# Five edits between the output projection and the experts of a hybrid encoder layer

## The reference, cut to what matters

```python
x = x + token_mixer(rmsnorm(x, attn_norm_g), w_in, ...)     # ends in  merged @ w_out
xn = rmsnorm(x, ffn_norm_g)
pg_top, g_sel = top_k(softmax(xn @ w_rg + b_rg), 1)         # 1 of 4 groups
pe_top, e_sel = top_k(softmax((xn @ w_re + b_re)[g_sel]), 2)  # 2 of its 8 experts
gate = pg_top * pe_top / sum(pe_top)
h = silu(xb @ w1[e]) * (xb @ w3[e])                         # 1024 -> 512
y = (h @ w2[e]) * gate                                      # 512 -> 1024
return rmsnorm(x + sum(y), final_norm_g)
```

## Time and profile before

| what | value |
|---|---|
| median of three runs | 1255.5 us |
| profiled execution, its time | 1254.98 us |
| profiled execution, its span | 1253.3 us |
| PE busy | 1114.9 us, 89% of the span |
| DVE busy | 510.9 us, 41% |
| ACT busy | 421.9 us, 34% |
| DMA moved | 308.89 MB |

### The profile page before, as it was taken

One profiled execution on the slowest core, in us unless ns is written; L12 is line 12 of the kernel. 1 busy time (PEld: TensorE's weight loads), 2 busy tenths in 40 slices (PEclk: granted clock), 3 DMA queues, 4 the chain that ended last, 5 costly groups with the idle time before them and its releaser, 6 DMA issues.

```text
span 1253.3 us, 15692 instructions
## 1 busy us (share of the span) xinstructions
PE 1114.9 (89%) x5136; PEld 684.8 (55%) x5136; DVE 510.9 (41%) x837; ACT 421.9 (34%) x658; POOL 229.9 (18%) x275
## 2 busy tenths in 40 slices
PE   5899999999988977999995699999999999898960
PEld 4688888888855645788784233333333333333320
DVE  5511111113237746755346244343515453424128
ACT  5322222223145655533114133333333342424222
POOL 0111101110007001000000033333323332423220
PEclk9899999999998967999996799999999999999985
DMA  8633331711160001746548989999999999999816
GB/s 320 233 118 118 112 114 50 284 47 45 50 252 2 1 1 42 246 133 241 195 158 331 420 340 375 419 420 419 421 419 365 421 420 420 420 420 420 336 36 276
DMA packets 69248, 308.89 MB, mean 246 GB/s; under 512 B 9025, under 2 KB 9153, under 8 KB 43873
## 3 DMA queue, kind: packets, MB, share of 16 engines
q1 hardware_dynamic: 56144, 273.86, 55.1%
q0 software_dynamic: 13072, 34.63, 7.2%
HBM read 278.57 MB, written 39.06 MB: 253 GB/s over the span
## 4 chain that ended last, share of the span: by engine, by line
PE 57%; DMA 22%; DVE 8%; ACT 6%; issue 5%; SPq 1%; DVEq 1%; ACTq 0%; POOLq 0%; POOL 0%
DMA rawe<-in_w 17%; PE ps L569 11%; PE ps L571 11%; PE ps L570 11%; PE ps L843 11%; PE ps L870 3%; ACT cur L1168 3%; PE ps L651 1%; DMA xres<-in_x_prompt 1%; PE ps L672 1%; PE ps L833 1%; DMA xrow<-in_x_sample 1%; DVE att L1316 1%; PE ps L684 1%; ACT prob L984 1%
## 5 line engine op out<-in xcount | busy, mean ns | idle before, releaser
L569 PE MATMUL ps<-whi,xTh 128*128 128x512 f32 x480 | 188.9, 394 | 18.5 <-DVE wlo L1199 14.0
L570 PE MATMUL ps<-wlo,xTh 128*128 128x512 f32 x480 | 188.5, 393 | 0.0
L571 PE MATMUL ps<-whi,xTl 128*128 128x512 f32 x480 | 188.2, 392 | 0.0
L843 PE MATMUL ps<-cur13a,xT 128*64 128x512 f32 x656 | 156.5, 619 | 25.9 <-DVEq L1601 25.1
L1199 DVE TENSOR_TENSOR wlo<-raw,whi 128x2048 fp32r<-128x2048 f32 x27 | 61.7, 2291 | 216.3 <-ACT whi L893 216.3
L843 PE MATMUL ps<-cur13b,xT 128*64 128x512 f32 x656 | 148.6, 592 | 0.0
L870 PE MATMUL ps<-cur,hT 128*64 128x512 f32 x640 | 146.2, 598 | 0.0
L1576 DVE COPY xT<-ps 128x512 f32<-128x512 f32 x41 | 28.3, 691 | 288.9 <-PE ps L833 288.9
L932 ACT ACTIVATE zst<-ps,rstd 128x512 f32<-128x512 f32 x60 | 41.3, 689 | 234.9 <-PE ps L571 232.8
L1168 ACT ACTIVATE cur<-rawe 128x4096 f32 x31 | 112.2, 3620 | 2.9 <-issue 0.2
L569 PEld LDWEIGHTS ps<-whi,xTh 128*128 128x128 f32 x480 | 91.1, 190 | 38.0 <-issue 18.8
(11 more groups left out here) (219 smaller groups left out, 1429.8 us busy)
## 6 DMA issues: line engine op xcount, KB each, us to landing
rawe<-in_w SPq DMA_DIRECT2D x96, 2048.0 KB
raw<-in_w_in SPq DMA_DIRECT2D x20, 1024.0 KB, 5.9
z_scratch<-zst POOLq DMA_DIRECT2D x60, 256.0 KB, 2.3
gat<-z_scratch SPq DMA_DIRECT2D x12, 512.0 KB, 3.7
xn_scratch<-rrow POOLq DMA_DIRECT2D x6, 1024.0 KB, 4.6
ya<-y_scratch SPq DMA_DIRECT2D x6, 1024.0 KB, 9.9
raw<-in_w_out SPq DMA_DIRECT2D x4, 1024.0 KB, 7.6
xcol<-in_x_cols SPq DMA_DIRECT2D x6, 512.0 KB, 10.2
```

The lines of the kernel that those rows point to most:

```text
L569: pe.matmul(out, ah, bh, start=first, stop=False)
L570: pe.matmul(out, ah, bl, start=False, stop=False)
L571: return pe.matmul(out, al, bh, start=False, stop=last)
L843: mm = pe.matmul(ps[0][u * CAP:(u + 1) * CAP, :], xT[:, c, h * CAP:(h + 1) * CAP], cur13[h][:, :, c * 512 + u * 256:c * 512 + u * 256 + 25 ...
```

## The change

- The residual gets three buffers in the place of old attention outputs. SP loads tiles 0 to 2 ahead of the first expert, and tile t+3 after the x2 store of tile t.
- The weights of position 1 are issued after the last product of the output projection, and the last x2 store behind them.
- In `next_up`, the copies to `cur13` stand ahead of the copy to `xT` and the hidden products. Each half waits for PE's half of up(b), for which there is a new semaphore `s_13a`.
- PE issues six products of 128 by 512 into a bank that nothing reads, between the last product of the block list and the wait for the list.
- `ORDER = (2, 0, 1, 3)` is the order of the groups in a round, for the weights, for the router's columns and for the ranks that decide ties.

```diff
+ORDER = (2, 0, 1, 3)
-    put("grank", NG - np.arange(NG))
+    put("grank", NG - np.array(ORDER))
-    xres = at("xres", F_O + 24 * KB, [P, D])
+    xres = [at(f"xres{s}", D_O + (20 + 4 * s) * KB, [P, D]) for s in range(3)]
...
-            for t in range(NT):
-                if t == 0:
-                    sp.wait_ge(s_mgd, 2 * NT)
-                else:
-                    sp.wait_ge(s_x2, 2 * t)
-                    x2_out(t - 1)
-                sp.dma_start(xres[:, :], x_tiles[t]).then_inc(s_xr, 16)
-                if t == 0:
-                    sp.wait_ge(s_lo, PRE)
-                    expert(0, 0)
+            def residual(t):
+                sp.dma_start(xres[t % 3][:, :], x_tiles[t]).then_inc(s_xr[t % 3], 16)
+            for t in range(3):
+                residual(t)
+            sp.wait_ge(s_lo, PRE)
+            expert(0, EPG * ORDER[0])
+            for t in range(NT - 1):
+                sp.wait_ge(s_x2, 2 * t + 2)
+                x2_out(t)
+                if t < 3:
+                    residual(t + 3)
+            sp.wait_ge(s_w, 2 * NT)
+            expert(1, EPG * ORDER[1])
             sp.wait_ge(s_x2, 2 * NT)
             x2_out(NT - 1)
-            sp.wait_ge(s_w, 2 * NT)
-            expert(1, 8)
             sp.wait_ge(s_rr, NT)
             for p in range(2, 8):
-                expert(p, EPG * (p % NG) + p // NG)
+                expert(p, EPG * ORDER[p % NG] + p // NG)
...
+            def keep_busy(n):
+                for _ in range(n):
+                    pe.matmul(ps[7][:, :], ident, C("rel")[:, 0:512], start=True, stop=True)
+            keep_busy(6)
             pe.wait_ge(s_nb, 1)
...
-                mm.then_inc(s_13, 1)
+                    mm.then_inc((s_13a, s_13)[h], 1)
...
             def next_up(b):
                 e, e1 = expert_of(dve, b), expert_of(dve, b + 1)
-                columns_of_rows(b + 1)
-                hidden(b)
                 with dve.If(e1 > e):
                     for k in (s_w1, s_w3):
...
+                    dve.wait_ge(s_c13, 2 * e1)
                     for h in range(2):
+                        dve.wait_ge((s_13a, s_13)[h], b + 1)
                         dve.tensor_copy(cur13[h][:, :, :], pair[:, :, h * PIECE:(h + 1) * PIECE]).then_inc(s_c13, 1)
+                columns_of_rows(b + 1)
+                hidden(b)
```

More of the change, by code:

```diff
@@ L310, in hybrid_layer @@
         s_mTl = sem("s_mTl")
-        s_xr = sem("s_xr")
+        s_xr = [sem(f"s_xr{s}") for s in range(3)]
         s_w = sem("s_w")
@@ L348, in hybrid_layer @@
         s_13 = sem("s_13")
+        s_13a = sem("s_13a")
         s_sge = sem("s_sge")
@@ L528, in _ @@
                 sp.sem_inc(k[2], 16)
-            for t in range(NT):
-                if t == 0:
-                    sp.wait_ge(s_mgd, 2 * NT)
-                else:
-                    sp.wait_ge(s_x2, 2 * t)
-                    x2_out(t - 1)
-                sp.dma_start(xres[:, :], x_tiles[t]).then_inc(s_xr, 16)
-                if t == 0:
-                    sp.wait_ge(s_lo, PRE)
-                    expert(0, 0)
+            def residual(t):
[11 more added lines that the diff above has]
+            expert(1, EPG * ORDER[1])
             sp.wait_ge(s_x2, 2 * NT)
             x2_out(NT - 1)
-            sp.wait_ge(s_w, 2 * NT)
-            expert(1, 8)
             sp.wait_ge(s_rr, NT)
             for p in range(2, 8):
-                expert(p, EPG * (p % NG) + p // NG)
+                expert(p, EPG * ORDER[p % NG] + p // NG)
             with sp.Fori(0, 2) as i:
                 for q in range(12):
-                    expert(12 * i + (8 + q), 3 * i + (EPG * (q % NG) + 2 + q // NG), (8 + q) % RING)
+                    expert(12 * i + (8 + q), 3 * i + (EPG * ORDER[q % NG] + 2 + q // NG), (8 + q) % RING)
             sp.wait_ge(s_c13, 2 * NE - 4)
@@ L1491, in _ @@
                     choose(0, NT - 2)
-                dve.wait_ge(s_xr, 16 * (t + 1))
+                dve.wait_ge(s_xr[t % 3], 16 * (t // 3 + 1))
                 for n in range(2):
@@ L1498, in _ @@
                     dve.tensor_tensor(x2[t % 3][:, n * 512:(n + 1) * 512], ps[6 + n][:, :],
-                                      xres[:, n * 512:(n + 1) * 512], ALU.add).then_inc(s_x2, 1)
+                                      xres[t % 3][:, n * 512:(n + 1) * 512], ALU.add).then_inc(s_x2, 1)
                 dve.wait_ge(s_sq2, t + 1)
@@ L1761 @@
     laid["x_cols"] = _np.ascontiguousarray(x.transpose(0, 2, 3, 1).reshape(NT, P, D))
+    order = list(ORDER)
     laid["router_w"] = _np.ascontiguousarray(_np.concatenate(
-        [inputs["w_rg"][0][:, None, :], inputs["w_re"][0].transpose(1, 2, 0)], axis=1).reshape(D, NG + NE))
+        [inputs["w_rg"][0][:, None, order], inputs["w_re"][0][order].transpose(1, 2, 0)], axis=1).reshape(D, NG + NE))
     laid["router_b"] = _np.ascontiguousarray(_np.concatenate(
-        [inputs["b_rg"][0][None, :], inputs["b_re"][0].T], axis=0).reshape(NG + NE))
+        [inputs["b_rg"][0][None, order], inputs["b_re"][0][order].T], axis=0).reshape(NG + NE))
     for name in _INS + list(laid):
```

## The result

The changed kernel took 1246.8 us, the median of six runs (1243.1 to 1247.2, and one disturbed execution of 2887 us, without which the median is 1246.5). The kernel before, run beside it, took 1254.6 us. The ratio, taken without the disturbed run, is 0.9928, 95% interval 0.9912 to 0.9944. So the gain is 8 us by the medians and 9 by the ratio. The profiled execution took 1247.24 us, its span is 1245.6 us. The forecast of 1246 and its sign hold. The sum behind it does not hold in every term.

A forecast was written before the change was run, and what follows sets the result against it. PE and the DMA weight queue were taken as within some per cent, the queue bounding the expert stage until position 28, PE after; -4.1 (output projection) and -5.1 (experts) gave -9.2, from 1255.5 to 1246 us, range 1241 to 1251.

The forecast's parts named there:

- Residual buffers, -4.1: Output projection: the stall for tile 1's residual goes, taken as -4.1 us, bounds 2.2 to 4.1 us gained.
- Position 1 ahead of the last store: End of output projection: weight stream starts 1.0 us earlier, nothing late behind the delayed store; bounds -1.0 to +3 us.
- Six products: PE before block 0: raised clock could save 3.3 us in blocks 0 and 1; bounds -3.3 to +2.3, counted only in part.
- Early copies: Expert changes: 11.75 us instead of 12.37, 31 times; after late weights, PE's first product follows 6.9 us later, before 2.50.
- 19 us of PE time: Expert stage: total PE time the early copies save over 31 changes of expert, where weights are there.
- Order: Expert stage: slots free later early on; last weight wait at position 28, with 5 blocks to the last up product, before 3.
- I take 10: Early expert stage: weight queue's dry time taken as 10 us, from 8.2 us, or 3.3 more at half clock.
- halfway between 1092.18 and 1157.16: Expert stage: arrival of position 28's weights in the old byte order, 1124.7 us, adjusted to 1123.2.
- the 5.1 of the middle: Expert stage: gain at the last up product, the middle between -6.6 and -3.5 us.
- A: Rival: dry time of 12 to 14 us and 7 us lag eat the expert gain; 1251 us, chance 0.21.
- B: Rival: dry time under 4 us as copies free slots 4.9 us earlier; 1239 to 1240 us, chance 0.10.
- C: Rival: POOL's gathers come late because of DVE's weight copies, making it slower, up to 1268 us; chance 0.07.

The follow-up runs named there:

- r1: The kernel before with only the three residual buffers added, last x2 store still ahead of position 1: 1250.93 us, ratio 0.9968 to before.
- a4: The changed kernel with the last x2 store put back ahead of the weights of position 1: 1246.49 us, ratio 0.9937 to before.
- a3: The changed kernel without the six unread products: 1247.09 us, ratio 0.9923 to before.
- r2: The kernel before with only the copies to cur13 moved ahead of xT and the hidden products: 1255.1 us, ratio 1.001 to before.
- a1: The changed kernel with DVE's copies back behind xT and the hidden products: 1246.12 us, ratio 0.9928 to before.
- a0: The changed kernel run again with no edit, as control: 1247.05 us, ratio 0.9937 to before.
- r3: The kernel before with only the new order of groups: 1250.95 us, ratio 0.9963 to before.
- c1: The changed kernel with w1 and w3 of the next position issued ahead of w2, from position 4 on: 1234.75 us, ratio 0.9844 to before.

## Why the prediction was right, and where its steps were not

1. *Residual buffers, -4.1.* Right, by the stores in the changed kernel and by r1 alone (4.0).
2. *Position 1 ahead of the last store.* The issue is 1.0 us earlier by its own step (656.56 against 663.13, less the 5.5 us by which all is earlier). ACT's copy starts at 678.39, expected 677.3 in this frame, and nothing is late behind it. The sum counts -1.0 for the step; a4 shows no effect.
3. *Six products.* The 7.55 us lie between the 5.2 and 10.3 of the two clock levels and are hidden: PE is idle 0.86 us behind them. The bound of +2.3, which is 10.3 less the wait of 7.95, was not reached. The gain of up to 3.3 us was rightly doubted. Block 0 gained its 1.75 us, block 1 did not, and a3 loses nothing without them. The 1244 us worked out from the rule of the Trainium skill (TensorE: Matmul & The Clock Gate, "Why this matters for your kernels") did not come.
4. *Early copies.* The mechanism and the sizes are right: 11.71 us a change (11.75), a lag of 6.51 us (6.9), a first half of 5.35 us. What the text did not draw out is that the "19 us of PE time" are worth, before the last late position, only what they take off the dry time (T1 3.0 us shorter in r2, 2.5 against a1). Behind it three changes gain 1.9 us, against 4.0 us of lag and 1.7 of slower pace. r2 and a1 show the edit at about zero.
5. *Order.* It is five block periods from the wait to the last up product, 58.56 us beyond the 1.7 of the slow half, forecast 58.75. The failed term is the arrival of position 28, forecast at 1123.2, measured at 1127.9 in the frame of before (1122.33 + 5.56). "I take 10" was 11.9 in this execution and 9.8 in a0, so it is a fair middle, with the higher value where block 1 runs at reduced clock, as the text had it. The rest is the interpolation: "halfway between 1092.18 and 1157.16" makes T1 less dry 1123.2 - 696.49 - 10 = 416.7, where this execution has 419.5, 2.8 us more, and all with this order have 419.0 to 420.4. The bytes point the same way. Before the change, the windows add up to 160.4 MB from the first up product to the late wait of position 26 and to 187.7 to that of position 30; halfway is 174.1. The changed kernel has moved 175.2 MB by position 28, and the seven executions with this order 174.5 to 175.6. That is 0.4 to 1.5 MB more than halfway, an estimated 1 to 4 us at 417 GB/s. Which transfers these are stays open.

So the expert stage gave 2.5 us (3.5 in a0) instead of the 5.1 of the middle. The 1.4 us of chance at the start of the span make the total of -7.7 look closer to -9.2 than the terms are. That the time came within 1 us of 1246 is in part luck: the 1255.5 us that the forecast starts from are the median of three runs, and six gave 1254.6.

*Rivals.* A had its conditions about met in this execution, dry time 11.9 us and a lag of 6.5 us, and yet did not come: the expert stage gave 2.5 us where A has none, and the order alone gives 4.6 us with 13.8 us of dry time (r3). B failed in the change but names the right lever: c1 brings dry time under 4 us and goes beyond B's time, because B saw only the dry time, and not the w2 in front. C did not happen. PE's waits in the loop, by what ended them (us in all, times, longest), are 16.4 us for the hidden rows, all but one of them behind late weights, and 1.8 us for gathers:

```profile
PE ps L861 <- DVE hh L1593: 16.4, 6, 4.2
PE ps L842 <- DMA xg<-xn_scratch,idxt: 1.8, 2, 0.9
```

Transposes wait for a gather twice, 1.8 us in all, both before the third block.

## What to carry to other kernels

Where a stream of weights and an engine are within some per cent of each other, split the stage at the last late arrival: an edit that saves engine time ahead of it is worth only what it takes off the queue's dry time, and what it adds between arrival and first product is paid in full. Before making consumers faster, look at the order in which one in-order queue waits for slots that free at different times. Putting the transfer whose slot frees first ahead of the one whose slot frees last was worth more here (12 us) than the five edits together (8 to 9 us).

## What the runs showed of the hardware

POOL's copy of one index column takes 1.59 us where it meets DVE's copy of weights (timeline of POOL), beside 0.18 us alone:

```profile
734.84 1.59 POOL L1719 COPY idxb<-idxt 128x1 int32 x1 [5.38 <-PE ps L842]
```

It ends at 736.43, DVE's copy of 'cur13b' at 736.39. The Trainium skill (SBUF — State Buffer, "SBUF: two separate sides") has that such a copy holds the shared port for its whole length. This row agrees: POOL is held until 0.04 us after the end of the copy, and the slack of the gathers covers it.

The granted clock is not the same in each execution of one kernel. Block 1's first half took 5.35 us in one profiled execution of the changed kernel (granted clock 0.74 between 700 and 705 us) and 3.65 us in the other (a0, 1.00 in the same window), behind the same six products. A gain of that size from products put in for the clock can't be read off a single profile. Over all fourteen it can: with the six products, 13 of the 18 first halves of blocks 0 and 1 took 3.65 us, and without them 2 of 10, the others 5.20 to 5.81. So the products mostly do keep the higher clock, and what they save is not seen in the time (a3). The clock also goes with the spread of the runs. Of the twelve runs of the kernel before beside c1, the one with the highest mean granted clock (0.956) took 1247.9 us and the one with the lowest (0.941) 1259.2. That is more than the whole gain of the change, so times are compared here as medians of several runs.
